# Two matmuls in place of three: high and low tokens in one matmul of 512 columns, two sums in a pair of banks

## The reference

```python
for layer in range(DEPTH):                       # DEPTH = 2
    h = rms_norm(x, norm_w[layer])
    proj = jnp.einsum('bsd,de->bse', h, w_in[layer])
    (a_xbc, a_z, a_dt, b_q, b_k, b_v, b_z,
     c_q, c_k, c_v, c_f, c_z, gates) = jnp.split(proj, split_at, axis=-1)
    y_a = mamba2_branch(a_xbc, a_z, a_dt, ...)
    y_b = sliding_window_branch(b_q, b_k, b_v, b_z, sinks[layer], cos, sin)
    y_c = forgetting_attention_branch(c_q, c_k, c_v, c_f, c_z, f_bias[layer])
    ys = jnp.stack([y_a, y_b, y_c], axis=2)
    branch = jnp.einsum('bsiw,iwd->bsid', ys, w_proj[layer])
    g = jax.nn.sigmoid(gates.reshape(b, s, N_BRANCH, d) + gate_bias[layer])
    x = x + jnp.einsum('bsd,de->bse', jnp.sum(g * branch, axis=2), w_out[layer])
return rms_norm(x, final_norm_w)
```

## Time and profile before

| | |
|---|---|
| median of 3 runs | 2228.97 us (2228.39 to 2231.36) |
| the profiled execution's own time | 2235.63 us |
| its span, first to last instruction | 2233.9 us |
| mean granted TensorE clock | 0.972 |
| busy: TensorE / VectorE / ScalarE / GpSimd | 2100.3 / 1258.7 / 1107.3 / 958.7 us |
| matmuls | 14868 |

### The profile page before, as it was taken

One profiled execution on the slowest core, in us unless ns is written; L12 is line 12 of the kernel. 1 busy time (PEld: TensorE's weight loads), 2 busy tenths in 40 slices (PEclk: granted clock), 3 DMA queues, 4 the chain that ended last, 5 costly groups with the idle time before them and its releaser, 6 DMA issues.

```text
span 2233.9 us, 36649 instructions
## 1 busy us (share of the span) xinstructions
PE 2100.3 (94%) x14868; PEld 1865.8 (84%) x14868; DVE 1258.7 (56%) x1902; ACT 1107.3 (50%) x1873; POOL 958.7 (43%) x426
## 2 busy tenths in 40 slices
PE   5999998999999998998999999899999979999997
PEld 5898997998998998996766787678888868898997
DVE  5576847336477655454276435555445546856665
ACT  4475466545575475544266323433333345646553
POOL 3564644563546644652111333323333333365663
PEclk9999999999999999998999999999999989999998
DMA  6445443566554543565112343433333313354551
GB/s 234 179 157 178 160 150 125 188 208 220 204 191 154 185 146 125 192 204 188 67 66 86 127 142 121 169 125 109 129 113 132 106 64 104 116 180 140 196 180 60
DMA packets 93176, 330.64 MB, mean 148 GB/s; under 512 B 10064, under 2 KB 13264, under 8 KB 92752
## 3 DMA queue, kind: packets, MB, share of 16 engines
q1 hardware_dynamic: 93008, 328.30, 42.7%
HBM read 327.08 MB, written 1.18 MB: 147 GB/s over the span
## 4 chain that ended last, share of the span: by engine, by line
PE 79%; DVE 10%; ACT 7%; issue 2%; POOL 1%; DMA 1%; SPq 0%; DVEq 0%; ACTq 0%; POOLq 0%
PE ps L797 22%; PE ps L798 21%; PE ps L799 21%; ACT t_hi L1145 2%; PE ps L844 2%; PE ps L810 1%; PE ps L811 1%; PE ps L812 1%; DVE t_lo L1454 1%; PE ps L933 1%; PE ps L1059 1%; PE ps L917 1%; DVE t_RB L1829 1%; PE ps L1069 1%; ACT t_B L1231 1%
## 5 line engine op out<-in xcount | busy, mean ns | idle before, releaser
L1925 POOL TENSOR_TENSOR t_lo<-t_raw,t_hi 128x1024 fp32r<-128x1024 f32 (+1 forms) x358 | 878.6, 2463 | 1078.6 <-ACT t_hi L1145 1070.5
L797 PE MATMUL ps<-t_RB,t_hi 128*128 128x256 f32 (+1 forms) x3712 | 1173.8, 316 | 20.5 <-DVE t_RB L1741 5.3
L798 PE MATMUL ps<-t_RB,t_hi 128*128 128x256 f32 (+1 forms) x3712 | 1151.2, 310 | 0.0
L799 PE MATMUL ps<-t_RB,t_lo 128*128 128x256 f32 (+1 forms) x3712 | 1150.5, 310 | 0.0
L797 PEld LDWEIGHTS ps<-t_RB,t_hi 128*128 128x128 f32 x3712 | 714.8, 193 | 94.2 <-issue 31.2
L798 PEld LDWEIGHTS ps<-t_RB,t_hi 128*128 128x128 f32 x3712 | 715.4, 193 | 34.9 <-issue 2.0
L799 PEld LDWEIGHTS ps<-t_RB,t_lo 128*128 128x128 f32 x3712 | 714.6, 192 | 35.8
L1145 ACT ACTIVATE t_hi<-t_raw 128x1024 fp32r<-128x1024 f32 (+1 forms) x506 | 524.5, 1042 | 426.9 <-PE ps L799 389.8
L1454 DVE TENSOR_TENSOR t_lo<-t_raw,t_hi 128x1024 fp32r<-128x1024 f32 x148 | 207.3, 1402 | 288.7 <-ACT t_hi L1145 288.5
L1884 DVE SCALAR_TENSOR_TENSOR t_A<-ps,t_V,t_A 128x510 f32<-128x510 f32 (+1 forms) x176 | 102.3, 612 | 154.6 <-ACT t_A L1415 153.1
L1415 ACT ACTIVATE t_A<-ps,t_V 128x512 f32<-128x512 f32 (+1 forms) x88 | 48.5, 577 | 125.9 <-PE ps L799 125.9
(11 more groups left out here) (302 smaller groups left out, 2180.5 us busy)
## 6 DMA issues: line engine op xcount, KB each, us to landing
t_raw<-in_W SPq DMA_DIRECT2D x586, 512.0 KB, 3.5
t_A<-cu_scratch SPq DMA_DIRECT2D x8, 512.0 KB, 6.1
t_B<-cu_scratch SPq DMA_DIRECT2D x8, 512.0 KB, 4.7
t_raw<-in_W SPq DMA_DIRECT2D x16, 256.0 KB, 2.9
t_A<-in_C SPq DMA_DIRECT2D x2, 1536.0 KB, 8.6
t_X<-in_X SPq DMA_DIRECT2D x2, 512.0 KB, 4.4
t_X<-in_X SPq DMA_DIRECT2D x1, 1024.0 KB, 9.9
out<-t_X SPq DMA_DIRECT2D x1, 1024.0 KB, 4.8
```

The costliest lines, as they stand in the source:

```text
L797: mm(o, hi[:, w], xh(k), start=k == 0 and j == 0, stop=False)
L798: mm(o, hi[:, w], xl(k), start=False, stop=False)
L799: i = mm(o, lo[:, w], xh(k), start=False, stop=k == nkt - 1 and m == u.x[1] - 1)
L1925: tt(t.lo[s][:, 0:w], t.raw[r][:, 0:w], t.hi[s][:, 0:w].bitcast(F), ALU.subtract).then_inc(*up("pool", ("split", u.i)))
```

## The change

In the first block the kinds q, k, vc, vb, rope, gate, proj, wout and z of branches 1 and 2 are now wide. The high and low parts of the tokens lie at a fixed distance from each other (the view `HX`, and `YX` for the branches' outputs), and so do the high and low parts of the weights (one tensor `hilo` in place of two). For each k-step and output tile, one matmul of 512 columns multiplies the high weights by both token parts, so that its bank holds high by high in columns 0 to 255 and high by low in columns 256 to 511; a second of 256 columns adds low by high to columns 0 to 255. In vc and vb the tokens are the stationary operand, and the 512 columns are high and low weights. A unit takes a pair of banks, one per output tile. ScalarE copies one half out (for z, gate and projection to the buffer where it is needed, or to a new buffer `PB`), and VectorE adds the other half. For wout VectorE adds both halves to x, one after the other. Silu and sigmoid become steps of their own: `zmul` one tick after z, `sig` one tick after the gate; `ysplit` of branches 1 and 2 comes a tick later than before. In the first block's layers `mod`, `rope2`, `gn_sum` and `small4` take side banks. conv, z of branch 0, the small projection and the second block compute as before.

```diff
@@ Order
     def bank(self):
-        self.ng += 1
-        return self.ng - 1
+        b, self.at = self.at, (self.at + 1) % 4
+        self.ng[b] += 1
+        return b, self.ng[b] - 1
+    def pair_of_banks(self):
+        self.at = (self.at + 1) // 2 * 2 % 4
+        return self.bank(), self.bank()
+    def zrest(self, l, c, br, n):
+        yield
+        self.add("zmul", l=l, c=c, n=n, x=(br,))
+        yield
+        self.add("ysplit", l=l, c=c, x=(br,))
...
@@ tensor
+    def wide(u, xx, point, *events):
+        for k in range(8):
+            q.wait_ge(point(k))
+            hi, lo = weights(u, k, 256)
+            for m in range(2):
+                b, w = gbank(u, m) if k == 0 else t.gb[u.g[m][0]], slice(m * 128, m * 128 + 128)
+                mm(b[:, :].rearrange("p (s t) -> p s t", s=2), hi[:, w], xx[:, :, k, :], start=k == 0, stop=False)
+                i = mm(b[:, 0:256], lo[:, w], xx[:, 0, k, :], start=False, stop=k == 7)
+            taken(u, i, k, 8, 256, ("mm", u.i, 0), *events)
...
     def rope2(u):
         q.wait_ge(at("roperaw", u.l, u.c))
-        b = gbank(u)
+        b = sbank(u)
...
@@ scalar
     def qk(u):
-        act(D[:, 2 * u.c:2 * u.c + 2, :], two(gbank(u)), ACT.Copy).then_inc(
-            *up("act", (u.kind, u.l, u.c), ("gfree", u.g[0])))
+        q.wait_ge(at("mm", u.i, 0))
+        act(D[:, 2 * u.c:2 * u.c + 2, :], t.ab(u)[0], ACT.Copy).then_inc(*up("act", (u.kind + "a", u.l, u.c)))
...
     def gate(u):
-        for m in range(2):
-            i = act(t.G[:, c % 2, m, :], b[:, m * 256:(m + 1) * 256], ACT.Sigmoid, bias=vec("gate_b", (l * 3 + br) * 8 + 2 * c + m))
-        i.then_inc(*up("act", ("gate", l, br, c), ("gfree", u.g[0])))
+        act(t.G[:, c % 2, :, :], t.ab(u)[1], ACT.Copy).then_inc(*up("act", ("gb", l, br, c)))
+    def sig(u):
+        q.wait_ge(at("gab", l, br, c))
+        for m in range(2):
+            g = t.G[:, c % 2, m, :]
+            i = act(g, g, ACT.Sigmoid, bias=vec("gate_b", (l * 3 + br) * 8 + 2 * c + m))
+        i.then_inc(*up("act", ("gate", l, br, c)))
+    def proj(u):
+        l, c, br = u.l, u.c, u.x[2]
+        q.wait_ge(at("mm", u.i, 0), was("pab", l, br, c - 1) if c else was("pab", l - (br == 2), {2: 1, 0: 2, 1: 0}[br], 3))
+        act(t.PB, t.ab(u)[1], ACT.Copy).then_inc(*up("act", ("pb", l, br, c)))
...
@@ vector
+    def qkv(u):
+        q.wait_ge(at(u.kind + "a", l, c))
+        tt(D, t.ab(u)[1], D, ALU.add).then_inc(*up("dve", (u.kind, l, c), ("gfree", *u.g[0]), ("gfree", *u.g[1])))
+    def gate(u):
+        q.wait_ge(at("gb", l, br, c))
+        tt(g, t.ab(u)[0], g, ALU.add).then_inc(*up("dve", ("gab", l, br, c), ("gfree", *u.g[0]), ("gfree", *u.g[1])))
...
     def proj(u):
-        ps, mg, G = two(t.gb[u.g[0] % 4]), t.MG[:, 2 * c:2 * c + 2, :], t.G[:, c % 2, :, :]
-        q.wait_ge(at("mm", u.i, u.x[0]), at("gate", l, br, c))
+        q.wait_ge(at("pb", l, br, c))
+        tt(ps, ps, t.PB, ALU.add).then_inc(*up("dve", ("pab", l, br, c)))
+        q.wait_ge(last(), at("gate", l, br, c))
...
     def wout(u):
-        tt(x, two(t.gb[u.g[0] % 4]), x, ALU.add).then_inc(
-            *up("dve", ("x", l + 1, 2 * c), ("x", l + 1, 2 * c + 1), ("gfree", u.g[0])))
+        a, b = t.ab(u)
+        tt(x, a, x, ALU.add).then_inc(*up("dve"))
+        q.wait_ge(last())
+        tt(x, b, x, ALU.add).then_inc(
+            *up("dve", ("x", l + 1, 2 * c), ("x", l + 1, 2 * c + 1), ("gfree", *u.g[0]), ("gfree", *u.g[1])))
```

More of the change, by code:

```diff
@@ L135, in small_cols, with is_wide @@
     return fn
+def is_wide(kind, x):
+    return kind in ("q", "k", "rope", "gate", "proj", "wout") or kind == "z" and x[-1] != 0
 @dataclass
@@ L246, in some_mods @@
                 self.open.append((l, c, 0))
-                self.add("mod", l=l, c=c, g=(self.bank(),))
+                self.add("mod", l=l, c=c, **self.one())
     def need_mods(self, l, j):
@@ L264, in gemm @@
             n = then(m0) if then else ()
-            self.add(kind, l=l, c=c, i=i, g=(self.bank(),), n=n, x=(m0, min(nm, m0 + per), *x))
+            g = self.pair_of_banks() if is_wide(kind, x) else (self.bank(),)
+            self.add(kind, l=l, c=c, i=i, g=g, n=n, x=(m0, min(nm, m0 + per), *x))
             if last and urgent:
@@ L324, in rest @@
             yield
-            self.add("small4", l=l, g=(self.bank(),))
+            self.add("small4", l=l, s=(self.sbank(),))
         self.side.append(rest())
@@ L332, in vproj @@
         self.split_after(i, 0)
-        self.add(kind, l=l, c=c, i=i, g=(self.bank(),))
+        self.add(kind, l=l, c=c, i=i, g=self.pair_of_banks())
         self.split_after(i, 1)
@@ L352, in gnorm @@
         for c in range(4):
-            self.add("gn_sum", l=l, c=c, g=(self.bank(),))
+            self.add("gn_sum", l=l, c=c, s=(self.sbank(),))
             yield
@@ L441, in g @@
             yield
-            self.add("rope2", l=l, c=c, g=(self.bank(),))
+            self.add("rope2", l=l, c=c, s=(self.sbank(),))
         self.side.append(g())
@@ L613, in __init__ @@
         self.gb, self.sb, self.d = T["gb"], T["sb"], T["d"]
+        self.pairs = [p[:, :].rearrange("p (m s t) -> p m s t", m=2, s=2) for p in T["pairs"]]
+        self.hilo = T["hilo"]
         E = T["E"]
```

179 lines of the change are left out of this document (116 added, 63 removed).

## The result

The changed kernel takes 2252.23 us (median of 4, 2250.13 to 2255.23) where the kernel before takes 2229.05 (2228.39 to 2231.36): ratio 1.0104, 95% interval 1.0089 to 1.0119, some 23 us more. The forecast was 2221 us with a range up to 2242; both the size and the sign are missed. The profiled execution is 2250.13 us (span 2248.4), 14.5 us longer than the profiled one of before.

What follows compares the result with a forecast made beforehand. TensorE's weight matmuls bound the pure stretches, while ScalarE and VectorE work holds much of the mixed ones. Terms -16.6 + 0 + 0.5 + 5 + 1.5 + 1.6 = -8.0 us gave 2221 us, 8-in-10 range 2207 to 2242.

Steps and rivals of the forecast that it cites:

- The price of a triple: Three weight matmuls of a k-step, 360 ns, become two at 346.7 ns; 16.6 us saved on the chain.
- Rival D: The mixed pair of matmuls still costs 360 ns, so nothing is saved and costs remain: 2238 us, chance 0.07.
- Pure stretches: 391 to 526 and 878 to 1000 us, TensorE the bound: copies and adds fit in idle time, cost 0.
- Fox stretches: 34 to 122 and 526 to 612 us: adds mostly fit in VectorE's waits, 0.5 us lost for both layers.
- turn: End of each layer: VectorE adds twice after the last output unit before the squares start, +1.5 us for two layers.
- last projection: Last projection to output, second layer: copy, semaphores and add enter the chain, +1.6 us; slack in the first layer.
- Mixed stretches: 183 to 391 and 670 to 878 us: 14 us of added work on the chain, less 9 us relief, net +5 us.
- z's product a tick later is free: z's multiply and split come one unit later; on branch 1 the split still meets its deadline, costed at nothing.
- Edits costed at nothing: Rotation, group-norm sums, small transposes and modulation in side banks stay hidden behind weight matmuls: 0, with 1 us in the range.
- The relief of 9 us: Mixed stretches: sigmoid and silu behind the bank's release take table loads off the chain, about 1.5 us at some six places.
- Rival C: Two pairs replace four banks; TensorE waits for held pairs at three places per layer, 21 us: 2242 us, chance 0.15.
- B: Rival: VectorE waits for copies behind exponentials, 14 us fall on the chain without the relief: 2231 us, chance 0.23.

Runs made afterwards that it cites:

- e2: The changed kernel with its 512-column matmul cut back into two of 256, pairs, adds, copies and moved silu and sigmoid kept: 2257.57 us, ratio 1.0120.
- e1: The changed kernel with high and low tokens of one k-step adjacent, so the 512 columns are one piece: 2250.2 us, ratio 1.0085.
- e12: e8 with the group-norm sums back in the matmul banks: 2242.47 us, ratio 1.0052.
- e3: The kernel before with only modulation, rope rotation, group-norm sums and small transposes moved to side banks, no pairs: 2238.05 us, ratio 1.0034.
- e8: The changed kernel with z of branch 2, rope and vb as before (one bank, three matmuls, no add): 2232.47 us, ratio 1.0009.
- e14: The changed kernel with only z of branch 2 as before (three matmuls in one bank, silu and product at once): 2239.05 us, ratio 1.0037.
- e10: The kernel before with only z of branches 1 and 2 and the gate copied out first, silu, sigmoid and z's product a tick later: 2233.82 us, ratio 1.0015.
- e9: The kernel before with only the group-norm sums moved to side banks: 2238.61 us, ratio 1.0033.
- e16: The changed kernel with all of branch 2, rope and vb as before and the group-norm sums in matmul banks: 2219.06 us, ratio 0.9951.
- e18: The changed kernel with branch 2's silu and product with y right after z's unit, pair, copy and add kept: 2249.82 us, ratio 1.0088.
- e17: e16 with the matmuls of a k-step in the order 512, 512, 256, 256: 2216.24 us, ratio 0.9937.

## Why the prediction was wrong

- **The price of a triple**, "I take 346.7": measured 353.7. The term was half of what I took. Both rows were right for a sequence of one size; "a sequence of either size alone runs as the line says" was used for a mixture, for which it does not hold in most units. -16.6 becomes about -8; e2 against e1 has 7.4, against the changed kernel 4. Rival D (nothing saved) was as far off on the other side. The 346.7 is a real pace all the same, in some units (e12); that I had no row for the mixture and took one value of two was the weak place.
- **Pure stretches, cost 0**: nearly right. Units start 5.65 us apart with no wait (forecast 5.55); 391 to 526 shrinks by 2.2 us, 878 to 993 by 1.1 (two units there start 0.6 and 0.3 us late), and not 4 to 5. Nearly all of that is the term above.
- **Fox stretches, turn, last projection**: right in one of four. From q 0 to the end of the block's first 122 us the changed kernel gains 1.1 us, as counted; in layer 2 it loses 0.3 where 2 were to be gained (k 1 starts 2.3 us late, once). Of the 1.5 us for the two turns nothing shows at the first, where the changed kernel gains 0.3 us; of the 1.6 for the last projection 0.3 shows.
- **Mixed stretches, net +5**: this is the step that failed. With their share of the saving I had +1 for both layers together; the unit starts show +12.4 and +8.9, 21 us. By the table 17.4 us are lost from z of branch 2 to rope 4 and 11.4 at the group-norm sums, which e3 loses without any pair; 4.7 come back between gate 1 and gate 2, and the rest is mostly what the matmuls save. I priced the adds by their duration (0.69 us each, 29 us in all) and by the share that VectorE holds of the chain. What they cost is where they stand: a bank that ScalarE could free at once is now freed behind a VectorE burst of 7 to 8 us. "Where ScalarE is late [...] VectorE now stands" names the coupling the other way round; here VectorE was late, and ScalarE and TensorE stood. e8 gives 21 us back, e14 15 of them.
- **z's product a tick later is free**: wrong. I looked only at branch 1 (window attention) and its deadline. In the forgetting attention's branch the token buffer is given back by that product, and ScalarE waits 7.19 us for it. The late operations alone (e10) cost 3.6 us net, the relief included.
- **Edits costed at nothing, side banks**: wrong by 7.5 us (e3, e9). I wrote "hidden behind weight matmuls" of the products and did not ask who else takes side banks, and when the reader of the sum comes.
- **The relief of 9 us**: half there at most. In the changed kernel it is 2.8 + 1.9 us (and e3 shows 2.3 of the first without it), in e16 10.8. The table loads are about as many as before (50 in the first 1000 us before, 51 after, 46 in e16); in e16 the gain came where one moved off the path to the evictions of attention. It was set off against a cost elsewhere, so that two errors would have had to cancel.
- **Rival C** (two pairs for four banks) had the right mechanism, at 0.15 and 2242 us, and a part of the places. Projection 0 of branch 0, one of its places, starts 3.3 us later against gate 1 in layer 1, which is C's 3.5, but by gate 2 this is won back; the rope stretch is where it stayed. B had the coupling. The chances followed a count of engine time, and that is why they were low. The 7.5 us of side banks stood in no rival.

Sum by runs: +21 (z, rope and v of the mixed stretches with what their own matmuls save), +7.5 (sums), -6 for the rest by difference (its matmuls and the relief, less its adds): 23. The parts come from different base kernels and need not add up (e12), so this is an account and not a proof.

Still open: why the same alternation of sizes takes 353 ns a triple in most units and 346.7 in some, and how the 15 us of z divide in layer 2 between the copy's wait and the held pair (in e18 both are on one add).

## What to carry to other kernels

An added instruction of 0.7 us is not priced by its duration, nor by its engine's idle share, but by the longest burst that can stand ahead of it in its queue and by who waits for what it frees. When a release moves from one engine to another, list the bursts of the new one. Then leave the change out where the release falls behind a burst: the same edit cost 23 us applied everywhere and gained 11 to 14 in e16 and e17, which leave out branch 2, rope and vb and keep the sums in matmul banks.

A buffer class into which something is moved has other users; ask for the last reader of each item in that class, and what that engine does just before.
